# A differential-attention phase whose two softmax maps are combined by TensorE instead of VectorE

## What is computed

```python
def diff_combine(s, lam):
    p = jax.nn.softmax(s, axis=-1)
    return p[..., 0, :, :] - lam * p[..., 1, :, :]
...
    def block(args):
        i, qi = args
        s = jnp.einsum('bqhmd,bkhmd->bhmqk', qi, k).astype(jnp.float32) * ATTN_SCALE
        ...
        attn = diff_combine(s, lam).astype(v.dtype)
        return jnp.einsum('bhqk,bkhe->bqhe', attn, v)
```

## Time and profile before

| what | value |
|---|---|
| median of 3 runs | 3633.48 us (3626.14 to 3634.31) |
| the profiled execution's own time | 3620.83 us |
| its span in the trace | 3619.1 us |
| busy over the span | PE 3310.7, DVE 1897.4, ACT 1443.0, POOL 1751.9 us |
| mean granted TensorE clock | 0.947 |

### The profile page before, as it was taken

The page is one execution under the profiler, slowest core; times in us unless marked ns, Lnnn a source line. Parts: engine busy times, 40 slices in busy tenths (PEclk is TensorE's granted clock), DMA queues, the critical chain, the costliest instruction groups (busy, mean ns, idle before and its releaser), DMA issues. The chain is left out here.

```text
span 3619.1 us, 78914 instructions
## 1 busy us (share of the span) xinstructions
PE 3310.7 (91%) x34073; PEld 3072.8 (85%) x34073; DVE 1897.4 (52%) x2177; ACT 1443.0 (40%) x2357; POOL 1751.9 (48%) x712
## 2 busy tenths in 40 slices
PE   7999968989897899999999999768887999999997
PEld 6798748888886899999999999545556999999997
DVE  6875364555555667563344332377644656741442
ACT  3434333343332334433333444355663443443342
POOL 3676500100010576666667666464203666666663
PEclk8999979999997899999999999888998999999998
DMA  8555443343334544455454566677645444544442
GB/s 287 168 168 178 151 162 102 114 141 122 126 121 135 178 140 135 130 149 152 139 155 140 177 192 186 187 247 277 252 158 187 135 138 139 141 141 141 138 144 84
DMA packets 784374, 575.21 MB, mean 159 GB/s; under 512 B 45290, under 2 KB 747522, under 8 KB 783772
## 3 DMA queue, kind: packets, MB, share of 16 engines
q1 hardware_dynamic: 728212, 506.00, 45.6%
q10 hardware_dynamic: 55816, 64.16, 5.4%
HBM read 499.80 MB, written 70.29 MB: 158 GB/s over the span
## 5 line engine op out<-in xcount | busy, mean ns | idle before, releaser
L1770 POOL TENSOR_TENSOR dense_w_lo<-w_raw,dense_w_hi 128x1024 fp32r<-128x1024 f32 x500 | 1282.5, 2570 | 920.9 <-ACT dense_w_hi L1858 634.3
L1827 PE MATMUL acc<-dense_x_hi,dense_w_hi 128*128 128x344 f32 x2448 | 773.6, 321 | 7.1 <-ACT dense_w_hi L1858 7.1
L1828 PE MATMUL acc<-dense_x_lo,dense_w_hi 128*128 128x344 f32 x2448 | 771.8, 320 | 0.0
L1858 ACT ACTIVATE dense_w_hi<-w_raw 128x1024 fp32r<-128x1024 f32 x504 | 530.5, 1055 | 502.8 <-PE acc L1832 441.3
L1827 PE MATMUL acc<-dense_hid_hi,dense_w_hi 128*128 128x344 f32 x1536 | 487.2, 322 | 0.0
L1828 PE MATMUL acc<-dense_hid_lo,dense_w_hi 128*128 128x344 f32 x1536 | 483.4, 319 | 0.0
L1827 PEld LDWEIGHTS acc<-dense_x_hi,dense_w_hi 128*128 128x128 f32 x2448 | 460.8, 188 | 8.4 <-ACT dense_w_hi L1858 6.4
L1828 PEld LDWEIGHTS acc<-dense_x_lo,dense_w_hi 128*128 128x128 f32 x2448 | 460.5, 188 | 0.6
L1832 PE MATMUL acc<-dense_x_hi,dense_w_lo 128*128 128x344 f32 x2496 | 445.1, 321 | 2.2 <-POOL dense_w_lo L1770 2.2
L1832 PEld LDWEIGHTS acc<-dense_x_hi,dense_w_lo 128*128 128x128 f32 x2496 | 405.5, 188 | 2.8 <-POOL dense_w_lo L1770 2.8
L864 POOL TENSOR_TENSOR x0T<-nT,levels 128x512 f32<-128x512 f32 x16 | 29.7, 1855 | 589.6 <-DVE bR L1534 589.6
(11 more groups left out here) (405 smaller groups left out, 6043.8 us busy)
## 6 DMA issues: line engine op xcount, KB each, us to landing
w_raw<-in_ffn_w SPq DMA_DIRECT2D x384, 512.0 KB, 4.2
proj_w_raw<-in_a_w_rkv SPq DMA_DIRECT2D x72, 512.0 KB, 4.4
att_k_page<-in_cache_k SPq DMA_DIRECT2D x64, 512.0 KB, 4.1
att_v_page<-in_cache_v SPq DMA_DIRECT2D x64, 512.0 KB, 5.5
w_raw<-in_ada_w SPq DMA_DIRECT2D x27, 1024.0 KB, 7.8
scratch_mix<-proj_stage ACTq DMA_DIRECT2D x72, 344.0 KB, 3.0
z<-scratch_mix SPq DMA_DIRECT2D x32, 512.0 KB, 9.1
ada_quarter<-in_ada_w SPq DMA_DIRECT2D x13, 1024.0 KB, 11.4
```

Of the source, the lines that this page charges most:

```text
L1770: nc.gpsimd.tensor_tensor(wlo[:, i % NW], raw[:, i % NRAW], whi[:, i % NW].bitcast(F32), ALU.subtract).then_inc(S("lo"), 1)
L1827: T_.matmul(out, whi[:, s % NW, k, :], a, start=j.first and k == 0, stop=False)
L1828: T_.matmul(out, whi[:, s % NW, k, :], b, start=False, stop=False)
L1858: A(whi[:, i % NW], raw[:, i % NRAW], ACT.Copy).then_inc(S("hi"), 1)
```

## The change

ScalarE's two exponentials stay apart until TensorE turns them. For each block of keys TensorE now makes two plain products into the same place in `tb`: the block of the first map with the identity, then the block of the second with a 128 x 128 diagonal of the ratios, accumulated. VectorE makes this diagonal once per unit from the identity, and no longer goes over the map. The maps' buffers become four deep (two kinds, two each), the combined map's buffers go, and the squares of the output are written over the causal mask's staging tile.

```diff
-        pm = (sb("probs_long", [P, 2, SEQ]), sb("probs_short", [P, 2, SEQ // 2]))
-        at = (sb("attn_long", [P, 2, SEQ]), sb("attn_short", [P, 2, SEQ // 2]))
+        pm = (sb("probs_long", [P, 2, 2, SEQ]), sb("probs_short", [P, 2, 2, SEQ // 2]))
+        ratio_diag = sb("ratio_diag", [P, 4, P])
...
-        o, osq, outT = sb("o", [P, 2, KC, P]), sb("o_sq", [P, P]), sb("out_cols", [P, SEQ])
+        o, osq, outT = sb("o", [P, 2, KC, P]), causal, sb("out_cols", [P, SEQ])
...
+            def turn_attn(name):
+                w, part = name[1], name[2]
+                need(pe, "t_in", nth[name])
+                for j in range(4 * part, min(4 * part + 4, blocks(w))):
+                    cols, out = slice(j * P, j * P + P), tb[:, (j - 4 * part) * P:(j - 4 * part + 1) * P]
+                    T_.matmul(out, probs_of(w, 0)[:, cols], m.ident[:], start=True, stop=False)
+                    last = T_.matmul(out, probs_of(w, 1)[:, cols], ratio_diag[:, w % 4, :], start=False, stop=True)
                 last.then_inc(S("t_mm"), 1)
...
                     need(pe, "attn", w + 1)
-                    turn4(("attn", w, 0), [attn_of(w)[:, j * P:j * P + P] for j in range(min(4, blocks(w)))])
+                    turn_attn(("attn", w, 0))
...
                 if live and blocks(w) > 4:
-                    turn4(("attn", w, 1), [attn_of(w)[:, j * P:j * P + P] for j in range(4, blocks(w))])
+                    turn_attn(("attn", w, 1))
                     values(w, 0)
...
-                V.scalar_tensor_tensor(attn_of(u)[:, 0:n], pm[kd][:, 1, 0:n], w1[:, c, 0:1], pm[kd][:, 0, 0:n], ALU.mult,
-                                       ALU.add).then_inc(S("attn"), 1)
+                V.tensor_scalar(ratio_diag[:, c, :], m.ident[:], w1[:, c, 0:1], None, ALU.mult).then_inc(S("attn"), 1)
...
                 need(act, "nb", u + 1)
-                need(act, "attn", u - 1)
+                if u >= 4:
+                    need(act, "t_mm", nth[attn_rounds(u - 4)[-1]] + 1)
```

More of the change, by code:

```diff
@@ L2146, in kind, with probs_of @@
             return u % 2
-        def attn_of(u):
-            return at[kind(u)][:, (u // 2) % 2]
+        def probs_of(u, mp):
+            return pm[kind(u)][:, (u // 2) % 2, mp]
         def pages_of(u):
@@ L2309, in turn4 @@
                 last.then_inc(S("t_mm"), 1)
+            def turn_attn(name):
[5 more added lines that the diff above has]
+                    last = T_.matmul(out, probs_of(w, 1)[:, cols], ratio_diag[:, w % 4, :], start=False, stop=True)
+                last.then_inc(S("t_mm"), 1)
             def head_rows(h, part):
@@ L2479, in combine @@
             def combine(u):
-                kd, c, n = kind(u), u % 4, blocks(u) * P
+                c = u % 4
                 need(dve, "exp", 2 * u + 2)
@@ L2584, in exps @@
             def exps(u, maps):
-                kd, c, n = kind(u), u % 4, blocks(u) * P
+                c, n = u % 4, blocks(u) * P
                 need(act, "nb", u + 1)
-                need(act, "attn", u - 1)
+                if u >= 4:
+                    need(act, "t_mm", nth[attn_rounds(u - 4)[-1]] + 1)
                 for mp in maps:
-                    A(pm[kd][:, mp, 0:n], scores_of(u, mp), ACT.Exp, bias=nb[:, c, mp:mp + 1],
+                    A(probs_of(u, mp)[:, 0:n], scores_of(u, mp), ACT.Exp, bias=nb[:, c, mp:mp + 1],
                       accum_out=l[:, c, mp:mp + 1]).then_inc(S("exp"), 1)
```

## The result

The changed kernel's median over four runs is 3655.48 us (3652.75 to 3662.13) against 3631.03 us for the kernel before (3626.14 to 3634.31): a ratio of 1.0071, 95% interval 1.0052 to 1.0090. It is slower by 0.7%. The profiled execution took 3656.52 us, with a span of 3654.7 us.

The account below looks back on a forecast made before the run. VectorE and GpSimd's ring was taken to bound early heads, TensorE heads 5 to 7. TensorE's 286 + 95 = 381 us, 393 at clock 0.97, plus 53 of pauses gave 446 against 423.4: 3655 us, range 3624 to 3688.

Parts of the forecast that it names:

- The price of the products: TensorE's turns in the attention: two plain products replace a transpose, adding 0.33 us per block, 95 us at full clock.
- The pauses and the clock: TensorE in the attention: pauses of 6 us per head plus 5 once, 53 us; clock 0.97, making 381 us 393.
- The distribution over heads: Attention by head: heads 0 to 2 gain slightly, to perhaps 47 to 51 us; heads 3 to 7 lose 4 to 6 each.
- The ring: Early heads: GpSimd's product, VectorE's page sum and combine wait on each other, then TensorE's turn; GpSimd's 66.1 us wait falls.
- VectorE's saving: VectorE in the attention: 64 diagonals of 19 us replace passes of 58.6 us, saving some 39 us, 4.9 per head.
- The faster case: Rival, heads 0 to 4: ring worth more than TensorE's added work; phase 410 us, 13 less; about 3620 us; chance 0.12.
- The case of an unchanged clock: Rival, attention: TensorE's mean clock stays at 0.86; phase 496 us, 73 us slower, 3706 us; chance 0.1.

Follow-up runs that it names:

- load_alone: Kernel before, with each block of the combined map turned by two plain products, one with the identity and one with zeros: 1.0116 times the kernel before.
- relief_alone: Changed kernel, but each first-map block turned by one transpose and the second map left out of the turned map: 0.9966 times the kernel before.
- four_transposes: Kernel before, with each block of the combined map transposed four times into the same place: 1.0106 times the kernel before.

## Why the prediction was right, and where it was not

**The price of the products** held, and with it the direction of the result: 0.22 us each against the 0.225 used, a turn of four at 1.96 us against 1.95. TensorE's work came to 381 us, the very sum that was forecast (286 + 95), and load_alone shows the same 381.

**The pauses and the clock** were choices, and came out close: pauses of 53 us against 53, clock 402.4 busy for 381 of work, which is 0.947 and not 0.97. That single term explains the phase's 455.5 us against the forecast 446. By the profiled executions the kernel is 36 us slower, 32 of them in the attention; by the medians it is 24 us slower, which is the forecast 22. The trace of before is of an execution of 3620.83 us, 10 us under the median, and that of the changed kernel is of one near its median. That the medians came out at 3655.48 us against a forecast of 3655 is therefore in part luck: measured as it was worked out, from trace to trace, the phase grew by 32 us and not by 22.

**The distribution over heads** was off. Heads 0 to 2 were to end at 47 to 51 us; they took 54.7, 46.0 and 53.3. Heads 5 to 7 were to lose 3 to 6 us; they lost 7.8, 6.9 and 9.0. Both errors go the same way; they did not cancel. The pauses were not the fault: they were 6.5 us per head in heads 5 to 7, against 6 chosen. In heads 0 and 2 it was the clock, 0.91 and 0.90 where 0.97 was chosen: head 2 needed 46.3 us for 41.7 of work. Head 0 paused for 13.1 us besides. In heads 5 to 7 the clock was close (0.97, 0.95, 0.97), but the prediction did not follow its own sum: with 12 us more work, 0.97 and 6 us of pauses it gives 57, 65 and 57 us, a loss of 5 to 7, for 58.9, 66.9 and 59.5 measured. It also gave each head the same 12 us. TensorE turns three units late, so its work rose by 8.8 us in the window of head 0 and by 14.7 in that of head 7.

**The ring** was half right. relief_alone and load_alone show that VectorE's relief is worth 12 to 16 us by the ratios; the traces put 7 to 9 us of it in the attention, in heads 0 to 4. But the wait that I took for its chief symptom, GpSimd's for the combine, was to fall and rose, from 91.9 us for both kinds of block to 106.6, and taking it away gained nothing: without it VectorE's passes are held up by GpSimd's products. TensorE's waits for the combine did go, from 17.5 to 5.3 us. The prediction also left out the longest wait in the attention, VectorE's 72.6 us for TensorE's scores. It lies in heads 5 to 7 for the most part (54.8 us), and it is there that the relief is worth nothing.

**VectorE's saving** of 39 us was 36: the diagonals took 22.6 us where 19 were forecast, at the upper bound given. One by itself takes 0.29 us, as chosen; the mean of 0.35 comes from those that met a product of GpSimd and took up to 0.73:

```profile
L2498 DVE TENSOR_SCALAR att_ratio_diag<-ident,att_ratio 128x128 f32<-128x128 f32 x64 | 22.6, 352 | 2.4 <-DVE att_ratio L2494 0.2
```

**The rivals.** The faster case needed pauses of 29 us in all; they were 53. The case of an unchanged clock fell: 0.947 against 0.86. The advice of the Trainium skill (Perfetto Trace Analysis, Transposes) to issue a logical transpose as a transpose is borne out, by 18 us for the first map alone. The statement of the Trainium skill (TensorE: Matmul & The Clock Gate, Part 4: PE-mode transpose) that transposes do not count as activity for the clock in the way matmuls do is contradicted for float32 by four_transposes, with 0.97, 0.95 and 1.00 in its last three heads against 0.90, 0.89 and 0.93 before.

## What to carry to other kernels

Work moved from a half-idle engine to the busiest one costs little as long as that engine still has pauses to fill (here 4 us for the first 34), and more than half of its price once they are filled (38 us for the next 61); so judge it stage by stage, and apply it only in the stages where the relieved engine holds the others up. A transpose can open an accumulation that a plain product continues, which makes a scaled sum of two transposed float32 blocks cost one transpose and one product. Before loosening a wait, look at what runs beside what without it.

## What the runs showed of the hardware

- A pass of VectorE over the maps or the identity in SBUF that starts during a product of GpSimd waits until the product ends and then does its work: 2.22 us for a pass of 0.35, and a median of 1456 ns for the diagonal of 286. By the Trainium skill (SBUF — State Buffer, Terms) the two engines share a port pair that is held exclusively for a whole instruction; both rows agree with it.
- A float32 transpose followed by an accumulating float32 product into the same place gave the scaled sum, and saved 36 us of TensorE's work over 288 blocks (381 against 345).
- TensorE's clock, as the mean over the attention, rose from 0.86 to 0.95 when its load rose by a third, with plain products (0.94 to 0.95) and with transposes (0.94) alike.
